# Beta/alpha product of a DeltaNet layer: activations as the stationary operand, 16 columns streamed

## The chip, the cores and the metric

One core of a Trainium2 chip runs the whole program. The metric is the device time in microseconds. Before the change the median of 3 runs was 1533.15 us, the lowest 1530.92 us and the highest 1536.06 us.

## The reference, cut to what matters

Two groups of tokens, 512 latent and 128 context tokens (640 together), pass two layers of a hybrid network of width 1024. The first layer has a bidirectional gated DeltaNet beside a short gated convolution, then a gated feed-forward part; the second has a pooling mixer and the same kind of feed-forward part. In the first layer one projection `w_in` feeds everything:

```python
p = h @ w_in                                  # h (tokens, 1024)
beta  = sigmoid(p[..., GATE_END:BETA_END])    # 2 directions x 4 heads = 8 columns
alpha = p[..., BETA_END:ALPHA_END]            # 8 columns
g = -exp(a_log) * softplus(alpha + dt_bias)
```

The change concerns these 16 columns only. All arrays are float32. `beta` and `g` are needed with one token per partition (five tiles of 128 tokens), because they scale and decay tokens of the scans.

## The kernel before, in words

Activations are kept with the channels on the partitions: `h` is eight blocks `k` of 128 channels by 640 tokens. To keep float32 accuracy each operand is split in two parts of the type fp32r: `hhi` and `hlo` for the activations, `whi` and `wlo` for the weights. A product is the sum of hi*hi, lo*hi and hi*lo over the eight blocks.

The projection is cut into 28 units of 128 output columns. A unit (`in_unit`, through `products`, L661 to L674) is 8 blocks x 3 part products x 2 halves of 320 tokens, so 48 matmuls whose stationary operand is a 128x128 piece of weights and whose moving operand is 320 tokens. The results alternate between the PSUM pairs A and B. While TensorE works on unit u, ScalarE takes the result of unit u-1 out of PSUM (L1085), VectorE runs the convolution over it (L1485 to L1494), and both split the weights of a later unit (L1098 and L1552). Each engine runs its own list of instructions in the order written, and semaphores tie the lists together; there is no planner.

The 16 beta/alpha columns have weights of their own, `wba_hi` and `wba_lo` (128 x 8 x 16). `beta_alpha` (L722) is issued on TensorE behind unit 5. It makes 48 matmuls with 16 columns of weights and 320 moving tokens, and leaves 16 partitions x 640 tokens in PSUM pair C. VectorE copies that to `acc` (L1561) between the work for units 5 and 6. Behind unit 7 TensorE transposes it in five pieces (`beta_alpha_tokens`, L732, the transposes stand on L736) into bank 7 of PSUM, 16 columns for each of the five token tiles. From there VectorE reads it (L1575, L1576) behind its loop over the first eight units, and the gate steps go on in `gates`. The semaphore `s_bat` counts the product, `s_gd` counts VectorE's gate steps (the copy is its first), `s_ba` says that bank 7 holds the result.

Behind the units 8 to 11 stand sums of squares for the q and k norms (`qk_sums`, L748). Behind unit 12 stand the gate sums (`gate_sums`, L759 and L761: six matmul records with 20 or 40 moving columns), and from unit 14 on products of k and q of one token tile (`grams`, L778) and decay rows (L768). A plain float32 matmul is one instruction in the code and two records in the trace.

Of the kernel before, what the change touches and what calls it, by code (L numbers as in the profile page):

```python
# [26 lines left out]
P = 128  # L27
D = 1024
KD = D // P
# [6 lines left out]
HALF = W // 2  # L36
# [11 lines left out]
TILES = [S0 + P * t for t in range(SEQ_S // P)] + [P0]  # L48
# [10 lines left out]
ALU = mybir.AluOpType  # L59
# [37 lines left out]
U_B, U_V, U_G = NQK, NQK + 3 * NB, NQKV + 3 * NB  # L97
BA_AFTER, GSUM_AFTER = 5, U_B + 4
# [46 lines left out]
def build(nc, t):  # L145
    ctx = ExitStack()
    with ctx:
        def sb(name, shape, dt=F32):
            return ctx.enter_context(nc.sbuf_tensor(name, shape, dt))

        def sem(name):
            return ctx.enter_context(nc.semaphore(name))
# [16 lines left out]
        wba_hi = sb("wba_hi", [P, KD, 16], F32R)  # L169
        wba_lo = sb("wba_lo", [P, KD, 16], F32R)  # L170
# [6 lines left out]
        ident, tri_u, tri_l, ones = (const[:, j, :] for j in range(4))  # L177
# [9 lines left out]
        acc = work[:, 8, :]  # L187
# [23 lines left out]
        hhi = nc.alloc_sbuf_tensor_at("hhi", [P, KD, W], F32R, offset=off_h)  # L211
        hlo = nc.alloc_sbuf_tensor_at("hlo", [P, KD, W], F32R, offset=off_h + size_h // 2)
# [48 lines left out]
        ps = ctx.enter_context(nc.psum_tensor("ps", [P, 8, 512], F32))  # L261
        pair = {n: ps[:, 2 * j:2 * j + 2, 0:HALF] for j, n in enumerate("ABCX")}
        bank = [ps[:, j, :].rearrange("p (h e) -> p h e", h=NH) for j in range(8)]

        def halves(ap):
            return ap.rearrange("p (b n) -> p b n", b=2)

        def col(name, pattern=None, **dims):
            a, n = COLS[name]
            v = cols[:, a:a + n]  # L270
            return v.rearrange(pattern, **dims) if pattern else v
# [76 lines left out]
        s_l2ln = sem("qk_logs")  # L348
        s_l2r = sem("qk_rsqrt")
        s_l2 = sem("qk_normed")  # L350
        s_bat = sem("beta_alpha_rows")
        s_ba = sem("beta_alpha_products")
        s_ga = sem("gate_steps_scalar")
        s_gd = sem("gate_steps_vector")
# [50 lines left out]
        def scan_tile(c, s):  # L405

            return NT - 1 if s == NT - 1 else (s if c == 0 else NT - 2 - s)

        def attn_of(n, c):

            return 2 * PREP.index(n) + c
# [248 lines left out]
        def _(pe):  # L660
# [56 lines left out]
            def in_unit(u, half_u, s, wait_k=None):  # L717
                pe.wait_ge(s_split, u + 1)
                pe.wait_ge(s_ev["AB"[s]], half_u + PRIMED)
                products("AB"[s], s, range(KD), hhi, hlo, range(KD), wait_k).then_inc(s_unit, 1)  # L720

            def beta_alpha():  # L722

                pe.wait_ge(s_mod, 1)
                for k in range(KD):
                    for q, (a, b) in enumerate(((wba_hi, hhi), (wba_hi, hlo), (wba_lo, hhi))):
                        for h in range(2):
                            last = nc.tensor.matmul(pair["C"][0:16, h], a[:, k, :], b[:, k, h * HALF:(h + 1) * HALF],
                                                    start=(k == 0 and q == 0), stop=(k == KD - 1 and q == 2))
                last.then_inc(s_bat, 1)  # L730

            def beta_alpha_tokens():  # L732

                pe.wait_ge(s_gd, 1)
                for tl, c0 in enumerate(TILES):
                    last = nc.tensor.transpose(ps[:, 7, 16 * tl:16 * tl + 16], acc[0:16, c0:c0 + P],  # L736
                                               ident[0:16, 0:16])
                last.then_inc(s_ba, 1)

            def qk_sums(m):  # L740

                pe.wait_ge(s_l2sq, m + 1)
                if m == 1:
                    pe.wait_ge(s_gd, 2)
                if m >= 2:
                    pe.wait_ge(s_l2ln, m - 1)
                for b in range(2):
                    last = nc.tensor.matmul(pair["CX"[m % 2]][:, b], ones, sq[m % 2][:, b * HALF:(b + 1) * HALF],  # L748
                                            start=True, stop=True)
                last.then_inc(s_l2sum, 1)  # L750
# [31 lines left out]
            for u in range(28):  # L782
                in_unit(u, u // 2, u % 2, (lambda j: pe.wait_ge(s_h, PRIMED + j + 1)) if u == 0 else None)
                if u == BA_AFTER:
                    beta_alpha()
                if u == U_B - 1:
                    beta_alpha_tokens()
                for m in L2_AFTER.get(u, ()):
                    qk_sums(m)
                if u == GSUM_AFTER:  # L790
                    gate_sums()
                if u in GRAMS_AFTER:
                    if GRAMS_AFTER[u] == 0:
                        pe.wait_ge(s_l2, 8)
                    for first in (4, 0):
                        grams(GRAMS_AFTER[u], first)
                if u in DECAYS_AFTER:
                    if DECAYS_AFTER[u] == 0:
                        pe.wait_ge(s_ga, 8)
                        pe.wait_ge(s_masks, 2)  # L800
                    for c in range(2):
                        decay_rows(DECAYS_AFTER[u], c)
# [65 lines left out]
            for s in range(NT):  # L868
                for c in range(2):
                    tl = scan_tile(c, s)  # L870
                    c0 = TILES[tl]
# [17 lines left out]
                    for h in range(NH):  # L889
                        last = nc.tensor.matmul(bank[b0 + 1][:, h], qkv[:, h, c0:c0 + P], S[:, h],  # L890
                                                start=True, stop=True)
                    last.then_inc(s_kq[c], 1)
                for c in range(2):
                    tl = scan_tile(c, s)
                    pe.wait_ge(s_r[c], s + 1)
                    for h in range(NH):
                        last = nc.tensor.matmul(bank[4 * c][:, h], rinv[:, 2 * tl + c, h], rr[c][:, h],
                                                start=True, stop=True)
                    last.then_inc(s_tr3[c], 1)
                for c in range(2):  # L900
                    tl = scan_tile(c, s)
# [6 lines left out]
                    for h in range(NH):  # L908
                        last = nc.tensor.matmul(bank[4 * c + 3][:, h], attn_kept[attn_of(tl, c)][:, h], vn[c][:, h],
                                                start=True, stop=True)  # L910
                    last.then_inc(s_ap[c], 1)

            for n in range(NT):
# [3 lines left out]
                for h in range(NH):  # L917
                    last = nc.tensor.transpose(bank[O_BANKS[n % 4]][:, h], osum[:, done_order[n], h], ident)
# [23 lines left out]
            for layer in range(2):  # L942
# [39 lines left out]
                for g, nf in enumerate(GROUPS):  # L982
                    b = SEG["up", layer, g]
# [401 lines left out]
        def _(dve):  # L1385
# [170 lines left out]
            dve.wait_ge(s_silu_rows, 1)  # L1556
            for u in range(NQK):
                s = u % 2
                if u == BA_AFTER + 1:
                    dve.wait_ge(s_bat, 1)  # L1560
                    nc.vector.tensor_copy(halves(acc)[0:16], pair["C"][0:16]).then_inc(s_gd, 1)  # L1561
                dve.wait_ge(s_ev["AB"[s]], u // 2 + (PRIMED + 1))
                dve.wait_ge(s_silu, u - s + PRIMED)
                conv(pad[s], cv[s], [tap_qkv[:, j, u:u + 1] for j in range(3)])
                weight_lo(u + 2)
                for _ in range(ROWS_IN[u]):
                    row_sums(rows)
                    rows += 1

            dve.wait_ge(s_ba, 1)  # L1570
            bav = ps[:, 7, 0:16 * NT].rearrange("p (t j) -> p t j", t=NT)

            def tiles(v):
                return v.rearrange("p (t j) -> p t j", t=NT)
            nc.vector.tensor_tensor(tiles(soft), bav[:, :, 8:16], tiles(col("dt_bias")), ALU.add)  # L1575
            nc.vector.tensor_scalar(tiles(lnbeta), bav[:, :, 0:8], -1.0, None, ALU.mult).then_inc(s_gd, 1)  # L1576

            def gate_logs():
# [208 lines left out]
            for s in range(NT):  # L1787
                for c in range(2):
                    tl = scan_tile(c, s)
                    dve.wait_ge(s_kq[c], s + 1)  # L1790
                    for h in range(NH):
                        j = tl * 8 + c * NH + h
                        last = nc.vector.scalar_tensor_tensor(
                            out=rr[c][:, h], in0=bank[4 * c][:, h], scalar=negegc[:, j:j + 1],
                            in1=vtok[:, tl, h], op0=ALU.mult, op1=ALU.add)
                    last.then_inc(s_r[c], 1)
                for c in range(2):
                    tl = scan_tile(c, s)
                    S = ss[:, c] if s < NT - 1 else sp_[:, c]
                    dve.wait_ge(s_ap[c], s + 1)  # L1800
                    for h in range(NH):
                        j = tl * 8 + c * NH + h
                        last = nc.vector.scalar_tensor_tensor(
                            out=S[:, h], in0=S[:, h], scalar=etot[:, j:j + 1], in1=bank[4 * c + 2][:, h],
                            op0=ALU.mult, op1=ALU.add)
                    last.then_inc(s_st[c], 1)
                for c in range(2):
                    tl = scan_tile(c, s)
# [28 lines left out]
            for n in range(NT):  # L1837
                c0 = TILES[done_order[n]]
# [25 lines left out]
            for layer in range(2):  # L1864
                if layer == 1:
# [6 lines left out]
                    for m in range(KD):  # L1872
                        dve.wait_ge(s_mix, m + 1)
                        for c0, n, cd in RANGES:
                            last = nc.vector.scalar_tensor_tensor(
                                out=x[:, m, c0:c0 + n], in0=ps[:, MIX_BANKS[m % 2][cd], 0:n],
                                scalar=mod[:, 1, 2, m, cd:cd + 1], in1=x[:, m, c0:c0 + n],
                                op0=ALU.mult, op1=ALU.add)
# [4 lines left out]
                for g, nf in enumerate(GROUPS):  # L1883
                    b = SEG["up", layer, g]
                    u, f = b["u"], b["f"]
# [169 lines left out]
```

## Time and profile before

| | |
|---|---|
| runs, median (lowest to highest) | 1533.15 us (1530.92 to 1536.06) |
| profiled execution, its own time | 1536.84 us |
| its span | 1535.0 us |
| TensorE matmul / weight load busy | 1411.7 us (92%) / 1371.1 us (89%) |
| VectorE, GpSimd, ScalarE busy | 980.9, 569.4, 433.5 us |
| mean granted TensorE clock | 0.974 |

The engines are named PE (TensorE matmul), PEld (TensorE weight load), DVE (VectorE), ACT (ScalarE), POOL (GpSimd). Matmuls are pipelined: the records of matmuls that follow each other overlap, so the time that one takes is read from the distance of the starts. In a merged row with a count, that distance is (length of the row less the length of one record) / (count less one). The granted clock is given as a share of 2.4 GHz; 0.50 is 1.2 GHz.

### The profile page before, as it was taken

The page shows a single profiled execution, that of the slowest core. Times are in us where ns is not written, and L with a number is a line of the kernel's source. Part 1 is how long each engine was busy: PE and PEld are TensorE (multiplying, and loading weights), DVE is VectorE, ACT ScalarE, POOL GpSimd, SP SyncE. Part 2 cuts the span into 40 slices and gives each one's busy share as a digit, 9 for nine tenths or more (in the row PEclk, how much of TensorE's full clock was granted, in tenths as well). Part 3 has the DMA queues.
Part 4 walks back from the last instruction along what each step waited for, and adds up shares of the span by engine and source line. Part 5 has one row for each costly group of instructions (what it writes and reads, how often), then busy time and mean ns, then how long its engine had stood idle before and what let it go on. Part 6 is the DMA issues. An engine that isn't in the chain of part 4 may idle for free.

```text
span 1535.0 us, 24664 instructions
## 1 busy us (share of the span) xinstructions
PE 1411.7 (92%) x9517; PEld 1371.1 (89%) x9517; DVE 980.9 (64%) x1403; ACT 433.5 (28%) x744; POOL 569.4 (37%) x348
## 2 busy tenths in 40 slices
PE   2699999989879799999999999897999999999995
PEld 1499989988878799999999999776999999999995
DVE  5774688887664677778888886445654155325554
ACT  4744442454421533101100111346331011001122
POOL 0200010003225355555556555212545454455542
PEclk9899999999999899999999999997999999999998
DMA  9242212353032245334344332111332222222222
GB/s 372 113 143 92 97 56 69 113 191 134 15 127 76 75 137 186 122 132 141 123 141 161 137 112 83 65 41 35 103 123 69 82 69 80 67 79 76 68 72 79
DMA packets 44791, 163.24 MB, mean 106 GB/s; under 512 B 4800, under 2 KB 5952, under 8 KB 43584
## 3 DMA queue, kind: packets, MB, share of 16 engines
q1 hardware_dynamic: 44736, 162.52, 30.5%
q8 instruction: 32, 0.52, 0.1%
q14 instruction: 23, 0.19, 0.0%
HBM read 154.12 MB, written 6.82 MB: 105 GB/s over the span
## 4 chain that ended last, share of the span: by engine, by line
PE 71%; DVE 15%; issue 6%; ACT 6%; DMA 2%; ACTq 0%; POOL 0%; DVEq 0%; SPq 0%; POOLq 0%
PE ps L670 61%; DVE ada_raw L1471 3%; PE ps L955 2%; DVE junk L1471 1%; DVE work L1488 1%; DVE work L1494 1%; ACT work L1024 1%; DVE work L1485 1%; ACT work L1170 1%; PE ps L682 1%; DMA x<-in_x 1%; DVE work L1893 1%; PE ps L778 1%; ACT work L1377 1%; DMA work<-in_zeros 1%
## 5 line engine op out<-in xcount | busy, mean ns | idle before, releaser
L670 PE MATMUL ps<-hhi,whi 128*128 128x320 f32 x1984 | 459.9, 313 | 40.5 <-DVE hlo L1455 31.6
L670 PE MATMUL ps<-hlo,whi 128*128 128x320 f32 x1984 | 454.4, 310 | 0.0
L670 PE MATMUL ps<-hhi,wlo 128*128 128x320 f32 x1984 | 454.0, 310 | 0.0
L599 POOL TENSOR_SCALAR whi<-raw 128x1024 fp32r<-128x1024 f32 (+1 forms) x146 | 161.0, 1103 | 621.0 <-PE ps L670 528.0
L602 POOL TENSOR_TENSOR wlo<-raw,whi 128x1024 fp32r<-128x1024 f32 (+1 forms) x146 | 374.5, 2565 | 12.2
L670 PEld LDWEIGHTS ps<-hhi,whi 128*128 128x128 f32 x1984 | 333.7, 190 | 50.0 <-issue 20.8
L670 PEld LDWEIGHTS ps<-hlo,whi 128*128 128x128 f32 x1984 | 334.5, 190 | 0.0
L670 PEld LDWEIGHTS ps<-hhi,wlo 128*128 128x128 f32 x1984 | 334.0, 189 | 0.0
L670 PE MATMUL ps<-hidhi,whi 128*128 128x320 f32 x704 | 161.3, 310 | 2.8 <-DVE hidlo L1896 2.8
L670 PE MATMUL ps<-hidlo,whi 128*128 128x320 f32 x704 | 161.1, 310 | 0.0
L670 PE MATMUL ps<-hidhi,wlo 128*128 128x320 f32 x704 | 161.1, 310 | 0.0
L1471 DVE SCALAR_TENSOR_TENSOR ada_raw<-ada_raw,cond_rows 128x1024 bf16<-128x1024 f32 x70 | 140.1, 2002 | 0.0
L1485 DVE TENSOR_SCALAR work<-work,cols 128x640 f32<-128x640 f32 x60 | 67.2, 1120 | 104.3 <-ACT work L1374 86.9
L670 PEld LDWEIGHTS ps<-hidhi,whi 128*128 128x128 f32 x704 | 118.5, 189 | 3.1 <-DVE hidlo L1896 3.1
L1374 ACT ACTIVATE work<-ps 128x640 f32<-128x640 f32 x44 | 31.0, 704 | 315.2 <-PE ps L670 315.0
L670 PEld LDWEIGHTS ps<-hidlo,whi 128*128 128x128 f32 x704 | 118.4, 189 | 0.0
L670 PEld LDWEIGHTS ps<-hidhi,wlo 128*128 128x128 f32 x704 | 118.4, 189 | 0.0
L1488 DVE SCALAR_TENSOR_TENSOR work<-work,cols 128x511 f32<-128x511 f32 x120 | 99.1, 866 | 3.7 <-DVE work L1485 0.3
L1896 DVE TENSOR_TENSOR hidlo<-work,hidhi 128x640 fp32r<-128x640 f32 (+1 forms) x44 | 74.5, 1693 | 41.2 <-ACT hidhi L1379 41.2
L1471 DVE SCALAR_TENSOR_TENSOR junk<-ada_raw,cond_rows 128x1024 bf16<-128x1024 f32 x70 | 90.5, 1292 | 1.9 <-DVE ada_raw L1471 0.5
L1426 DVE SCALAR_TENSOR_TENSOR x<-ps,mod,x 128x320 f32<-128x320 f32 (+2 forms) x120 | 45.4, 434 | 71.6 <-PE ps L670 71.6
L1377 ACT ACTIVATE work<-work 128x640 f32<-128x640 f32 x44 | 32.5, 739 | 198.6 <-DVE work L1494 198.4
(205 smaller groups left out, 1353.1 us busy)
## 6 DMA issues: line engine op xcount, KB each, us to landing
raw<-in_w_gu SPq DMA_DIRECT2D x88, 512.0 KB, 3.2
ada_raw<-in_w_rows SPq DMA_DIRECT2D x70, 512.0 KB, 3.6
raw<-in_w_in SPq DMA_DIRECT2D x28, 512.0 KB, 3.3
raw<-in_w_dn SPq DMA_DIRECT2D x32, 448.0 KB, 3.4
ada_first<-in_w_ada SPq DMA_DIRECT2D x4, 2048.0 KB, 22.6
raw<-in_w_dn SPq DMA_DIRECT2D x16, 512.0 KB, 3.3
row_late<-in_w_rows SPq DMA_DIRECT2D x10, 512.0 KB, 3.3
raw<-in_w_out SPq DMA_DIRECT2D x8, 512.0 KB, 4.2
```

The lines of the kernel that those rows point to most:

```text
L599: nc.gpsimd.tensor_scalar(whi[s][:, 0:n], raw[s][:, 0:n], 1.0, 0.0, ALU.mult, ALU.add).then_inc(s_whi, 1)
L602: nc.gpsimd.tensor_tensor(wlo[s][:, 0:n], raw[s][:, 0:n], whi[s][:, 0:n].bitcast(F32), ALU.subtract).then_inc(s_split, 1)
L670: last = nc.tensor.matmul(pair[pr][:, b], wt[s][:, cs], act[:, k, b * HALF:(b + 1) * HALF], start=(j == 0 and q == 0), stop=(j == len(tile ...
L682: last = nc.tensor.matmul(ada_row(n), c_parts[:, q, 4 * s + k, :], w[:, k * ADA_COLS:(k + 1) * ADA_COLS], start=(s == 0 and k == 0 and q = ...
L955: last = nc.tensor.matmul(ps[:, bk, 2 * P * e:2 * P * (e + 1)], h_mix[:, 2 * g + kk, at:at + P], w_mix[:, g, kk, :], start=(kk == 0), stop ...
L1374: nc.scalar.activation(halves(pad[0]), pair["A"], ACT.Copy).then_inc(s_ev["A"], 1)
L1377: nc.scalar.activation(cv[1], cv[0], ACT.Silu).then_inc(s_silu, 1)
L1426: last = nc.vector.scalar_tensor_tensor(out=x[:, k, xc:xc + ln], in0=pair[n][:, bk, pc:pc + ln], scalar=mod[:, layer, 3 * part + 2, k, cd: ...
L1471: last = nc.vector.scalar_tensor_tensor(out=(row_out(n), row_buf(n)[:, 0:SLOT // 2].bitcast(mybir.dt.bfloat16))[c], in0=row_buf(n), scalar ...
L1485: own.tick(nc.vector.tensor_scalar(dst[:, 0:W], src[:, 0:W], taps[1], None, ALU.mult))
L1488: last = nc.vector.scalar_tensor_tensor(out=dst[:, c0 + 1:c0 + n], in0=src[:, c0:c0 + n - 1], scalar=taps[0], in1=dst[:, c0 + 1:c0 + n], o ...
L1896: nc.vector.tensor_tensor(hidlo[:, i, :], h32[0], hidhi[:, i, :].bitcast(F32), ALU.subtract).then_inc(s_hid, 1)
```

## The change

`beta_alpha` now takes a piece of the activations, 128 channels x 128 tokens, as the stationary operand and streams the 16 columns of `wba_hi` or `wba_lo`. Each of the five token tiles takes 8 blocks x 3 part products, 120 matmuls together, and writes its 16 columns of bank 7 directly, with tokens on the partitions. `beta_alpha_tokens`, VectorE's copy and the semaphore `s_bat` are gone. The first of VectorE's two gate steps (the addition of `dt_bias`) raises `s_gd` in place of the copy, so that the later counts stay as they were.

```diff
@@ -722,19 +721,11 @@
             def beta_alpha():
 
                 pe.wait_ge(s_mod, 1)
-                for k in range(KD):
-                    for q, (a, b) in enumerate(((wba_hi, hhi), (wba_hi, hlo), (wba_lo, hhi))):
-                        for h in range(2):
-                            last = nc.tensor.matmul(pair["C"][0:16, h], a[:, k, :], b[:, k, h * HALF:(h + 1) * HALF],
+                for tl, c0 in enumerate(TILES):
+                    for k in range(KD):
+                        for q, (b, a) in enumerate(((hhi, wba_hi), (hlo, wba_hi), (hhi, wba_lo))):
+                            last = nc.tensor.matmul(ps[:, 7, 16 * tl:16 * tl + 16], b[:, k, c0:c0 + P], a[:, k, :],
                                                     start=(k == 0 and q == 0), stop=(k == KD - 1 and q == 2))
-                last.then_inc(s_bat, 1)
-
-            def beta_alpha_tokens():
-
-                pe.wait_ge(s_gd, 1)
-                for tl, c0 in enumerate(TILES):
-                    last = nc.tensor.transpose(ps[:, 7, 16 * tl:16 * tl + 16], acc[0:16, c0:c0 + P],
-                                               ident[0:16, 0:16])
                 last.then_inc(s_ba, 1)
@@ -783,8 +774,6 @@
                 if u == BA_AFTER:
                     beta_alpha()
-                if u == U_B - 1:
-                    beta_alpha_tokens()
@@ -1556,9 +1545,6 @@
                 s = u % 2
-                if u == BA_AFTER + 1:
-                    dve.wait_ge(s_bat, 1)
-                    nc.vector.tensor_copy(halves(acc)[0:16], pair["C"][0:16]).then_inc(s_gd, 1)
                 dve.wait_ge(s_ev["AB"[s]], u // 2 + (PRIMED + 1))
@@ -1572,7 +1558,7 @@
-            nc.vector.tensor_tensor(tiles(soft), bav[:, :, 8:16], tiles(col("dt_bias")), ALU.add)
+            nc.vector.tensor_tensor(tiles(soft), bav[:, :, 8:16], tiles(col("dt_bias")), ALU.add).then_inc(s_gd, 1)
```

## Rows read from the trace of the kernel before

**Rows 1.** The page: shares of the chain of work that ended last.
```profile
PE 71%; DVE 15%; issue 6%; ACT 6%; DMA 2%; ACTq 0%; POOL 0%; DVEq 0%; SPq 0%; POOLq 0%
```

**Rows 2.** That chain in order of time, 113 to 145 us: start, length, what.
```profile
113.60 7.03 PE ps L728 x48
120.63 14.08 PE ps L670 x96
134.71 0.41 PE ps L736 x5
135.12 7.24 PE ps L670 x48
```

**Rows 3.** Busy time by engine around the product: stretch, length, busy (records), clock.
```profile
113.30:120.50 7.20, 7.20 (x52) 4.74 (x51) 3.83 (x8) 2.39 (x3) 0.00 (x0) 1.00 0.44 139
120.50:127.60 7.10, 7.10 (x50) 7.10 (x50) 0.81 (x1) 0.00 (x0) 0.00 (x0) 1.00 0.06 23
```

**Rows 4.** VectorE in order of time: start, length, operation, idle before it.
```profile
120.67 0.81 DVE L1561 COPY work<-ps 16x640 f32<-16x640 f32 x1 [2.50 <-PE ps L728]
128.44 0.56 DVE L1485 TENSOR_SCALAR work<-work,cols 128x640 f32<-128x640 f32 x1 [6.96 <-ACT work L1085]
139.19 0.20 DVE L1575 TENSOR_TENSOR gates<-ps,cols 128x40 f32<-128x40 f32 x1
```

**Rows 5.** Who TensorE waited for, 105 to 300 us: total, times, longest.
```profile
PE ps L778 <- DVE qkv L1597: 2.5, 1, 2.5
```

**Rows 6.** Weight loads by shape: busy, mean ns of one.
```profile
L670 PEld LDWEIGHTS ps<-hhi,wlo 128*128 128x128 f32 x1984 | 334.0, 189 | 0.0
...
L728 PEld LDWEIGHTS ps<-hhi,wba_hi 128*16 128x16 f32 x16 | 1.5, 95 | 0.8
...
L769 PEld LDWEIGHTS ps<-below,ident 128*128 128x128 bf16 x10 | 1.0, 98 | 2.4 <-issue 2.4
```

**Rows 7.** Weight loads in order of time, clock 1.00, three places.
```profile
368.51 0.97 PEld L887 LDWEIGHTS ps<-ss,qkv 128*128 128x128 f32 x8 [1.51 <-issue]
...
178.83 0.56 PEld L759 LDWEIGHTS ps<-gates,const 128*128 128x128 f32 x4
179.31 0.30 PEld L761 LDWEIGHTS ps<-gates,const 128*128 128x128 f32 x2
179.53 0.30 PEld L670 LDWEIGHTS ps<-hhi,whi 128*128 128x128 f32 x2
...
134.63 0.39 PEld L736 LDWEIGHTS ps<-const,work 16*128 16x128 f32 x5 [0.19 <-issue]
```

**Rows 8.** Weight loads in order of time, at clock 0.50.
```profile
198.59 3.39 PEld L778 LDWEIGHTS ps<-qkv 128*128 128x128 f32 x16 [2.81 <-DVE qkv L1597]
```

**Rows 9.** Stretches that end as the clock falls, and some behind them.
```profile
196.05:198.40 2.35, 0.00 (x0) 0.00 (x0) 2.35 (x4) 2.35 (x10) 0.00 (x0) 1.00 0.62 223
198.60:201.80 3.20, 3.20 (x15) 3.20 (x16) 2.30 (x3) 1.22 (x3) 0.00 (x0) 0.50 0.04 12
201.80:205.00 3.20, 3.20 (x15) 2.01 (x15) 2.84 (x8) 2.59 (x10) 1.64 (x2) 1.00 0.42 152
...
494.17:498.78 4.61, 1.35 (x5) 0.68 (x4) 0.10 (x1) 4.31 (x6) 2.52 (x2) 1.00 0.19 52
...
498.78:505.60 6.82, 1.15 (x4) 1.18 (x5) 4.51 (x6) 5.60 (x10) 0.00 (x0) 0.50 0.50 196
...
1030.98:1034.67 3.69, 1.13 (x4) 0.68 (x4) 2.63 (x5) 0.96 (x2) 0.00 (x0) 1.00 0.00 0
...
1517.51:1522.78 5.27, 1.35 (x4) 0.68 (x4) 0.09 (x1) 4.99 (x7) 0.00 (x0) 1.00 0.01 2
```

**Rows 10.** Dense stretches at clock 0.50 until it rises, and one behind.
```profile
504.45:509.02 4.57, 4.54 (x16) 4.14 (x17) 3.95 (x6) 4.34 (x9) 0.00 (x0) 0.50 0.00 0
...
1045.71:1051.74 6.03, 5.93 (x21) 5.53 (x22) 5.09 (x7) 5.66 (x11) 0.00 (x0) 0.50 0.00 0
1051.74:1056.00 4.26, 3.00 (x17) 2.21 (x15) 2.37 (x4) 4.07 (x8) 0.00 (x0) 1.00 0.02 4
```

More of the change, by code:

```diff
@@ L350, in build @@
         s_l2 = sem("qk_normed")
-        s_bat = sem("beta_alpha_rows")
         s_ba = sem("beta_alpha_products")
```

## The prediction

> **What bounds the kernel now.** I read the shares of the chain first: TensorE holds 71% of the chain that ended last [rows 1]. Then the chain in order of time around the changed place [rows 2]: it never leaves TensorE from the product (7.03 us, 48 matmuls) over two units (14.08 us) and the five transposes (0.41 us) into the next unit. The busy times say the same: TensorE fills all 7.20 us and 7.10 us of the two stretches at clock 1.00, while VectorE works 3.83 and 0.81 us and ScalarE 2.39 and 0.00 us [rows 3]. The list of waits has for TensorE between 105 and 300 us one entry, 2.5 us [rows 5]. So what TensorE gains or loses behind unit 5 goes to the end one for one, unless a later wait takes it up. That one wait is for VectorE's norm of q and k, which hangs on sums issued on TensorE behind units 8 to 11, so it moves along with TensorE and takes up nothing.
>
> **The change part by part.**
>
> *Removed on TensorE:* the product, 7.03 us; the transposes, 0.41 us; and the slower start of the unit behind them, 7.24 us [rows 2] where 14.08 / 2 = 7.04 us is usual, so 0.20 us. Together 7.64 us. TensorE's wait for VectorE's copy lies within these.
>
> *Removed on VectorE:* the copy, 0.81 us. It is worth nothing: VectorE waited 2.50 us before it and 6.96 us behind it, the latter for unit 6's result [rows 4]. The readers of bank 7 (L1575, at 139.19 us) stand behind the loop over eight units and come some 4 us after the transposes were done, so that the result's being ready earlier brings nothing either; they wait for nothing new. The moved count of `s_gd` holds: the sums for the second q tile need the value 2, which both gate steps now give together. No DMA is added or moved, and SyncE's and GpSimd's lists keep their order.
>
> *Added on TensorE:* 120 pairs of a weight load (128 columns) and a matmul with 16 moving columns. In the old product one pair took 7.03 / 48 = 0.146 us and the matmul's 320 columns set it. With 16 columns the load must set it. A load of fp32r weights with 128 columns is recorded with 189 ns, with 16 columns 95 ns [rows 6], so 94 ns for 112 columns, 0.84 ns each, or 107 ns for 128. The distance of the starts agrees: eight float32 loads with 128 columns in 0.97 us make (0.97 - 0.19) / 7 = 0.111 us; and the nearest rows by moving columns, six pairs with 20 or 40 of them, take from 178.83 to 179.53 us, 0.117 us each [rows 7]. So a pair costs 0.111 us at the full clock, taking the longer series of equal pairs. The bounds from rows at that clock: below, the loads of the transposes, (0.39 - 0.14) / 4 = 0.062 us a pair [rows 7], with 16 rows; above, the 0.146 us of today. They give 7.4 and 17.6 us for the 120; 0.111 gives 13.3 us.
>
> Were the clock to stay at 1.00, the sum would be 13.3 - 7.64 = +5.7 us.
>
> *The clock.* It does not stay, I think. The rows before four of the trace's nine falls from 1.00 to 0.50 (2.4 GHz to 1.2) show TensorE with few moving columns: no matmul for 2.35 us, or four or five records in 3.69 to 5.27 us, 1.13 to 1.35 us of it busy [rows 9]. In the new product the array streams 16 columns each 0.111 us, where a unit streams 320 each 0.147 us: 7% of the columns of today, over 13 us. Only the weight loads would be dense. The trace has no stretch with dense loads and sparse columns, so whether loads alone hold the clock up is open, and I bound it from both sides: not at all (+5.7 us) and at 0.50 throughout.
>
> At 0.50 sixteen loads take (3.39 - 0.19) / 15 = 0.213 us each [rows 8], so 120 pairs take 25.6 us. The clock does not fall at once. The rows put the fall 2.35 to 5.27 us behind the last dense work; the four mean 4.0 us. By then 4.0 / 0.111 = 36 pairs are done, and the other 84 take 84 x 0.213 = 17.9 us: 21.9 us together (20.5 to 23.5 us for the ends). Then unit 6 begins at 0.50. The rows show dense work at 0.50 for 3.2, 4.57 and 6.03 us until the clock rises [rows 9, 10]; the mean is 4.6 us and half of it, 2.3 us, is lost (1.6 to 3.0 us). The sum: 21.9 + 2.3 - 7.64 = +16.6 us, with ends 20.5 + 1.6 - 7.6 = +14.5 and 23.5 + 3.0 - 7.6 = +18.9 us.
>
> The Trainium skill bears on this in "TensorE: Matmul & The Clock Gate", Part 4 (PE-mode transpose): it says that transposes do not count as PE-busy in the way that makes the chip give the full clock. Its "What's actually happening" has activity release the throttle, without saying that weight loads are activity. No row here tests loads alone; if a load counts like a matmul, the sum is the +5.7 us above, if it doesn't, the +16.6 us.
>
> Forecast: the profiled execution's 1536.84 us becomes 1553.4 us. The median of the runs lies 3.7 us below that execution, and against it the time is 1533.15 + 16.6 = 1549.8 us.
>
> **The rivals.**
>
> *A: the dense loads hold the clock at 1.00.* For it: TensorE is never idle in the product, and the falls in the rows all come with much idle time. Against it: before three of those four falls TensorE was not wholly idle [rows 9], and a load moves no columns. It gives +5.7 us, 1538.8 us (up to +10 us if a pair costs 0.146 us).
>
> *B: not slower.* One mechanism: the fp32r loads of the new product go faster than 0.111 us a pair. From 7.64 / 120 = 0.064 us down the change is no loss. For it: loads with 128 columns and 16 rows come each 0.062 us, and a bf16 load with 128 columns is recorded with 98 ns, hardly over one with 16 columns [rows 6, 7]. Against it: these have another type or few rows, and the same activations' type as weights (L670) shows 189 ns. At 0.062 us it gives 7.4 - 7.64 = -0.2 us, 1533 us, if the shorter stretch also spares the clock. The skill's section "Fast Weight Load" of the same page says that the fast load needs a type other than FP32, which would speak against B if fp32r counts as FP32; and its "Back-to-back issue gap" has about 81 ns for a sustained pair with 128 columns, which would give 9.7 us for the 120, +2.1 us; the 0.111 us of the trace stand against that.
>
> *C: the pairs cost more than a load.* If fp32r with few moving columns is run as two passes with two loads, as a plain float32 matmul is, 240 loads come to 26.6 us at 1.00 and up to 51 us at 0.50: +19 to +46 us, 1552 to 1579 us. For it: each float32 instruction has two records. Against it: the old product's 48 fp32r matmuls have 48 records [rows 2], with 320 columns each.
>
> **How the numbers follow.** The clock falls: 0.68. A: 0.19. B: 0.05. C: 0.08. The likeliest gives 1550 us, its own range 1546 to 1555 us (the ends +14.5 and +18.9 us, and some 2 us for the spread of a median over the runs, 1530.92 to 1536.06). The 8-in-10 range goes down to A: 1537 to 1556 us; it leaves out B, most of C and A's lowest edge. A measurement of this kernel can tell about 0.3%, 4.6 us, from no change. A's +5.7 us lies near that bound, so a third of A counts as the same, with B's greater part: same 0.10, faster 0.03, slower 0.87.
>
> **What would show it.** In the new profile the product should be 120 matmul records with 128x16 moving, none of L736 or L1561. The clock shown for that stretch should be 1.00 for its first 2.4 to 5.3 us, with load starts 0.11 us apart, then 0.50 with 0.213 us. The whole should take some 22 us, and unit 6 behind it over 7.04 us. VectorE's wait for unit 6's result should grow from 6.96 us by the same amount. TensorE's wait before L778 should stay near 2.5 us. If the clock stays at 1.00 throughout, A holds. If loads stand under 0.1 us apart at 1.00, B. If there are 240 records, C. If the product takes 22 us and the time does not grow by some 14 us, the claim that nothing behind it takes up the delay is wrong.

## The result

The changed kernel takes 1551.3 us (median of 4 runs, 1546.88 to 1551.88) where the one before took 1534.4 us in the same runs (1530.92 to 1536.06): a ratio of 1.0107, 95% interval 1.0080 to 1.0134, so it is slower by some 16 us. In the profiled execution of the changed kernel, which took 1546.88 us, its span 1545.1 us, TensorE's mean granted clock is 0.967 (0.974 before).

The chain that ended last shows the place. This is that chain of the changed kernel, in order of time: start, length, what.

```profile
113.00 22.66 PE ps L727 x120
135.65 23.15 PE ps L669 x144
```

The product (now L727) takes 22.66 us where it took 7.03 [rows 2]. The three units behind it (L669, 144 matmuls; nothing stands between the second and the third any longer) take 23.15 us, where three units at the full clock take 21.1.

The clock shows why. The first view has the busy time by engine and the granted clock (third number from the end) of four stretches of the changed kernel; the second its weight loads where the clock falls: start, length, operation.

```profile
112.83:115.89 3.06, 3.06 (x31) 3.06 (x29) 2.05 (x4) 1.65 (x2) 0.00 (x0) 1.00 0.64 216
115.89:135.65 19.76, 19.76 (x95) 19.76 (x94) 1.67 (x3) 0.74 (x1) 0.00 (x0) 0.50 0.08 27
135.65:139.79 4.14, 4.14 (x17) 4.14 (x17) 0.00 (x0) 0.00 (x0) 0.00 (x0) 0.50 0.02 4
139.79:145.00 5.21, 5.21 (x37) 5.21 (x36) 0.00 (x0) 0.23 (x1) 0.00 (x0) 1.00 0.00 0
```

```profile
115.74 0.19 PEld L727 LDWEIGHTS ps<-wba_hi,hhi 128*128 128x128 f32 x1
115.85 0.29 PEld L727 LDWEIGHTS ps<-wba_hi,hlo 128*128 128x128 f32 x1
116.02 0.34 PEld L727 LDWEIGHTS ps<-wba_lo,hhi 128*128 128x128 f32 x1
116.24 0.33 PEld L727 LDWEIGHTS ps<-wba_hi,hhi 128*128 128x128 f32 x1
116.45 0.33 PEld L727 LDWEIGHTS ps<-wba_hi,hlo 128*128 128x128 f32 x1
```

For 3.06 us from the product's first matmul (112.83 us) the loads come 0.111 us apart at 2.4 GHz. Then the clock goes to 1.2 GHz, the recorded load from 0.19 to 0.33 us, and the distance to 0.213 us. TensorE counts as 100% busy in all four stretches, before the fall and behind it: the busy share alone says nothing here, and the clock beside it says everything. The clock comes back 4.14 us after the units began again. VectorE and ScalarE have next to nothing to do in 24 us; VectorE's wait for unit 6's result is now 27.95 us.

```profile
145.50 0.56 DVE L1474 TENSOR_SCALAR work<-work,cols 128x640 f32<-128x640 f32 x1 [27.95 <-ACT work L1074]
```

The wait grows by 21.0 us. Before, the copy parted it into 2.50 us, the copy's own 0.81 us and 6.96 us [rows 4], 10.3 us together; against these the growth is 17.7 us, which is the longer product (15.6 us) and the slower unit 6 (2.0 us).

Compared by the ends of units, unit 5 ends 0.6 us earlier than in the trace of before, and unit 8 ends 16.4 us later: the place costs 17.0 us in the profiled execution. That execution was the fastest of four. By its own time it is only 10.0 us over the profiled execution of before, for reasons that lie elsewhere in the program (last section).

### The profile page after: what moved, and what is told of

The parts are those of the page before. It is cut to its first block, busy times and chain, and to the rows that moved or that the text cites. A ratio compares the mean times of both kernels' runs of the same rounds, so it can differ in the third digit from the quotient of the medians.

```text
span 1545.1 us, 24797 instructions
## 1 busy us (share of the span) xinstructions
PE 1428.6 (92%) x9584; PEld 1390.8 (90%) x9584; DVE 975.9 (63%) x1402; ACT 433.4 (28%) x744; POOL 569.9 (37%) x348
## 4 chain that ended last, share of the span: by engine, by line
PE 71%; DVE 15%; ACT 5%; issue 5%; DMA 1%; ACTq 0%; POOL 0%; DVEq 0%; SPq 0%; POOLq 0%
PE ps L669 60%; DVE ada_raw L1460 3%; PE ps L944 1%; DVE junk L1460 1%; PE ps L727 1%; DVE work L1477 1%; DVE work L1483 1%; DVE work L1474 1%; ACT work L1013 1%; ACT work L1159 1%; PE ps L681 1%; DVE work L1879 1%; PE ps L769 1%; DMA x<-in_x 1%; ACT work L1366 1%
## 5 line engine op out<-in xcount | busy, mean ns | idle before, releaser
L669 PE MATMUL ps<-hhi,whi 128*128 128x320 f32 x1984 | 460.5, 314 | 38.5 <-DVE hlo L1444 31.3
L669 PE MATMUL ps<-hlo,whi 128*128 128x320 f32 x1984 | 455.1, 311 | 0.0
L669 PE MATMUL ps<-hhi,wlo 128*128 128x320 f32 x1984 | 454.8, 310 | 0.0
L669 PEld LDWEIGHTS ps<-hhi,whi 128*128 128x128 f32 x1984 | 334.9, 190 | 47.6 <-issue 20.8
L669 PEld LDWEIGHTS ps<-hlo,whi 128*128 128x128 f32 x1984 | 335.4, 190 | 0.0
L669 PEld LDWEIGHTS ps<-hhi,wlo 128*128 128x128 f32 x1984 | 334.9, 190 | 0.0
L669 PE MATMUL ps<-hidhi,whi 128*128 128x320 f32 x704 | 160.5, 309 | 0.1
L669 PE MATMUL ps<-hidlo,whi 128*128 128x320 f32 x704 | 160.4, 309 | 0.0
L669 PE MATMUL ps<-hidhi,wlo 128*128 128x320 f32 x704 | 160.3, 309 | 0.0
L1474 DVE TENSOR_SCALAR work<-work,cols 128x640 f32<-128x640 f32 x60 | 63.8, 1063 | 126.8 <-ACT work L1363 88.3
L1460 DVE SCALAR_TENSOR_TENSOR ada_raw<-ada_raw,cond_rows 128x1024 bf16<-128x1024 f32 x70 | 136.2, 1946 | 0.0
L669 PEld LDWEIGHTS ps<-hidhi,whi 128*128 128x128 f32 x704 | 117.8, 188 | 0.3 <-DVE hidlo L1882 0.3
L669 PEld LDWEIGHTS ps<-hidhi,wlo 128*128 128x128 f32 x704 | 117.9, 188 | 0.0
L669 PEld LDWEIGHTS ps<-hidlo,whi 128*128 128x128 f32 x704 | 117.7, 188 | 0.0
L1477 DVE SCALAR_TENSOR_TENSOR work<-work,cols 128x511 f32<-128x511 f32 x120 | 105.1, 917 | 3.7 <-DVE work L1474 0.3
```

Source lines behind the costliest of these rows:

```text
L669: last = nc.tensor.matmul(pair[pr][:, b], wt[s][:, cs], act[:, k, b * HALF:(b + 1) * HALF], start=(j == 0 and q == 0), stop=(j == len(tile ...
L1460: last = nc.vector.scalar_tensor_tensor(out=(row_out(n), row_buf(n)[:, 0:SLOT // 2].bitcast(mybir.dt.bfloat16))[c], in0=row_buf(n), scalar ...
L1474: own.tick(nc.vector.tensor_scalar(dst[:, 0:W], src[:, 0:W], taps[1], None, ALU.mult))
L1477: last = nc.vector.scalar_tensor_tensor(out=dst[:, c0 + 1:c0 + n], in0=src[:, c0:c0 + n - 1], scalar=taps[0], in1=dst[:, c0 + 1:c0 + n], o ...
```

## The experiments

All ran beside the kernel before, whose median was 1534.7 us in the first four and 1535.3 us in the other three.

**The changed kernel once more**, with no edit.

> The changed kernel once more, beside the kernel before. Theory (the clock falls in the stretch of bare weight loads): some 17 us over the kernel before; in the profile the 120 pairs take 20.5 to 23.5 us, their load starts 0.111 us apart until the granted clock goes to 0.50, and 0.213 us from there on, the fall standing 2.3 to 5.3 us into the product. Rival (the fall seen once was a chance of that execution): a clock of 1.00 through the product, 13.3 us for it and +5.7 us.

Measured: 1550.7 us, ratio 1.0107 (1.0088 to 1.0126). The chain, and by it the product:

```profile
115.18 21.14 PE ps L727 x120
136.31 23.05 PE ps L669 x144
```

The clock stands at 1.00 for the first 4.73 us of the product and at 0.50 from there to 3.92 us into unit 6:

```profile
115.02:119.75 4.73, 4.73 (x46) 4.73 (x44) 3.72 (x6) 2.39 (x3) 0.00 (x0) 1.00 0.42 138
119.75:136.31 16.56, 16.56 (x80) 16.56 (x79) 0.00 (x0) 0.00 (x0) 0.00 (x0) 0.50 0.10 32
136.31:140.23 3.92, 3.92 (x16) 3.92 (x16) 0.00 (x0) 0.00 (x0) 0.00 (x0) 0.50 0.01 4
```

In the other execution the fall stood at 3.06 us; 1.6 us more at 0.111 us a pair spare 1.5 us of the whole. So the cost differs with the place of the fall, within the range expected: from the product's start to the end of unit 8 this execution takes 15.4 us more than before, the other 17.0 us. Both traces have the fall.

**Eight times the columns.** Each matmul streams its 16 columns eight times over:

```diff
-last = nc.tensor.matmul(ps[:, 7, 16 * tl:16 * tl + 16], b[:, k, c0:c0 + P], a[:, k, :],
+last = nc.tensor.matmul(wide[tl], b[:, k, c0:c0 + P],       # wide: (r=8, j=16) of bank 7 or 6
+                        a[:, k, :].unsqueeze(1).to_broadcast([P, 8, 16]),
```

> The changed kernel with the same 120 loads, but each matmul streams its 16 columns eight times over (128 moving columns, into eight columns groups of PSUM of which the first is read). Nothing else differs but four small reads in place of two. Theory (the clock falls because few columns are streamed): the added columns fit under a load (about 0.05 us of streaming in 0.111 us), the clock stays at 1.00, the product takes 13.3 us instead of 22.7 and the kernel is 5.7 us over the one before, so about 11 us under the changed one although it streams eight times the columns. Rival (a long series of fp32r loads is slow or drops the clock by itself): no gain over the changed kernel, +17 us, and the clock at 0.50 in the product.

Measured: 1538.6 us, ratio 1.0032 (1.0017 to 1.0047) to the kernel before: some 12 us faster than the changed kernel, with the same loads and more arithmetic. The chain of this kernel and the clock of the product:

```profile
112.45 13.35 PE ps L729 x120
125.80 21.17 PE ps L669 x144
```

```profile
112.30:125.60 13.30, 13.30 (x122) 13.30 (x121) 3.71 (x6) 2.39 (x3) 0.00 (x0) 1.00 0.27 90
```

The product takes 13.35 us, 0.111 us a pair, the units behind it 21.17 us, and the clock is 1.00 throughout. Weight loads as dense as in the changed kernel did not drop the clock; with them dense in both, what differs is how many columns the matmuls move and, with them, how many results they write. No run parts these two. This is the run that parts the two terms of the sum: 120 loads instead of 48 matmuls, and the clock.

**The pairs beside dense matmuls**, one behind each matmul of units 5 to 7:

```diff
@@ products
                             last = nc.tensor.matmul(pair[pr][:, b], wt[s][:, cs], ...)
+                            if beside is not None:
+                                beside()                     # one load and one 16-column matmul
@@ the loop over units
-                if u == BA_AFTER:
-                    beta_alpha()
+                in_unit(..., ba_pair if u >= BA_AFTER else None)
```

> The changed kernel with the same 120 pairs, one behind each matmul of units 5 to 7 in place of all behind unit 5. Theory (a pair costs its load, 0.111 us at the full clock, and the 11 us on top are the clock's): the unit's dense matmuls beside keep it at 1.00, units 5 to 7 take 3 x 7.04 + 13.3 = 34.4 us, and the kernel is 5.7 us over the one before. Rival 1 (loads hide under the unit's matmuls, which have 0.036 us each to spare): units 5 to 7 take under 30 us and the kernel is faster than before by up to 2 us. Rival 2 (not the clock): +17 us as the changed kernel.

Measured: 1541.2 us, ratio 1.0052 (1.0032 to 1.0072), so +8 us with an interval from 5 to 11. The clock over the three units and the loads within one:

```profile
105.00:139.50 34.50, 34.50 (x267) 34.50 (x266) 16.09 (x28) 7.18 (x9) 0.00 (x0) 1.00 0.29 100
```

```profile
109.91 0.19 PEld L669 LDWEIGHTS ps<-hhi,whi 128*128 128x128 f32 x1
110.02 0.19 PEld L730 LDWEIGHTS ps<-wba_hi,hhi 128*128 128x128 f32 x1
110.17 0.19 PEld L669 LDWEIGHTS ps<-hhi,whi 128*128 128x128 f32 x1
```

From one load of the unit to the next there are 0.26 us, as much as 0.147 for the unit's matmul and 0.111 for the pair: the pair costs its full price beside the unit's matmul, although that leaves 0.036 us beyond its own load. Why nothing of it hides was not tried. From the first matmul of unit 5 to that of unit 8 there are 34.3 us (105.39 to 139.73), where 34.4 us were expected and the kernel before, transposes included, has 28.65 us (106.40 to 135.05): 5.7 us more. The first rival is out, and the second by the clock.

**The old product twice**: `for _ in range(2):` around the old layout's loops, 48 dense matmuls more at the same place.

> The kernel before with its product computed twice, 96 matmuls of 320 columns, so 7.03 us more of dense TensorE work at the same place and no change of the clock. Theory (what TensorE gains or loses there goes to the end one for one): +7.0 us. Rival (a later wait takes part of it up): +0 to +5 us, and TensorE's waits behind unit 8 are shorter in the profile than before.

Measured: 1542.1 us, ratio 1.0043 (1.0027 to 1.0059), so +6.6 us, from 4.1 to 9.1. In its profile the units from 6 on lie 7.2 us later than before, 0.2 us of which was there ahead of the product, and what stands behind the scans lies 6.8 us later. TensorE's waits behind unit 8, and the second of them as the kernel before has it:

```profile
PE ps L779 <- DVE qkv L1598: 2.5, 1, 2.5
PE ps L839 <- DVE work L1688: 2.2, 1, 2.2
```

```profile
PE ps L838 <- DVE work L1687: 3.2, 1, 3.2
```

The first is as it was [rows 5]. The second, in the scans, is 1.0 us shorter, which is the rival's sign; but the delay behind the scans is only 0.3 to 0.4 us less. Nearly all of it is passed on, and the rival's 0 to 5 us are left only in the part from 4.1 us up.

**Two products beside**: the run before last, with the hi activations loaded once for hi and lo weights.

```diff
-ba_pairs = [... for k in range(KD) for q in range(3)]
+ba_pairs = [... for k in range(KD) for q in range(2)]
-                b, a = ((hhi, wba_hi), (hlo, wba_hi), (hhi, wba_lo))[q]
+                b, n = ((hhi, 32), (hlo, 16))[q]             # moving: wba[:, k, 0:n]
```

> The change's layout with its pairs beside the matmuls of units 5 to 7 as in the run before it, and with two products in place of three: the hi activations stay loaded and stream 32 columns, the hi and the lo weights side by side, the lo activations stream 16, and VectorE adds the two parts. 80 pairs in place of 120. Theory (the price of this layout is the number of its loads, 0.111 us each at the full clock): units 5 to 7 take 21.1 + 8.9 = 30.0 us, and the kernel is 8.9 - 7.64 = 1.2 us over the one before, 4.4 us under the kernel with 120 pairs beside. Rival (the price is the streamed columns or something fixed): no nearer to before than that kernel, +5 to +8 us.

Measured: 1534.3 us, ratio 0.9998 (0.9985 to 1.0012). From the first matmul of unit 5 to that of unit 8 its profile has 29.9 us (104.67 to 134.59), the clock at 1.00 throughout. That is 4.4 us less than with 120 pairs beside (34.3) and 1.3 us more than before (28.65), both as expected. By the medians, forty loads fewer brought more, 8.3 us (both intervals taken together, about 4.6 to 12); the profiles show 4.4 of it at this place. So the layout of the change, with the clock kept and a third of the loads gone, is as fast as the kernel before, and no faster.

**The old product within unit 0**, whose blocks wait for the split activations:

```diff
+BA_BLOCKS = {2: (0,), 3: (1, 2), 4: (3,), 5: (4, 5), 7: (6, 7)}   # behind block j of unit 0
-                if u == BA_AFTER:
-                    beta_alpha()
```

> The kernel before with its own layout, where the product's blocks are computed between the blocks of unit 0, in which TensorE waits for the split activations: block 0 behind block 2 of the unit, 1 and 2 behind 3, 3 behind 4, 4 and 5 behind 5, 6 and 7 at the end. Theory (time of TensorE counts one for one where it is never idle, and less where it waits): the 48 matmuls fill gaps of 0.3 to 1.2 us each; worked out block by block from the starts in the trace, unit 0 and the product end some 3.4 us after the end of unit 0 today and not 7.03 us, so 3.6 us faster than before. Rival (the gaps are not free because the later blocks are held up as well): 0 to 2 us faster.

Measured: 1532.5 us, ratio 0.9985 (0.9971 to 1.0000), some 2.3 us faster, at most 4.5. The 3.6 us lie in the interval, and so does all of the rival; not settled by the time. The profile has no wait of TensorE left inside unit 0 except the one before its first block. From the first matmul of unit 0 to that of unit 8 it has 66.2 us (61.37 to 127.56), before 69.3 us (65.71 to 135.05): 3.1 us less, nearer to the 3.6 us than to the rival's 0 to 2. That is one execution of each kernel, with the clock at 0.50 for the first 4.7 us of this stretch here and 3.0 us before.

**The same with two products**, 32 weight columns (hi and lo) against the hi activations and 16 against the lo:

```diff
-for q, (a, b) in enumerate(((wba_hi, hhi), (wba_hi, hlo), (wba_lo, hhi))):
+for q, (n, b) in enumerate(((32, hhi), (16, hlo))):
     for h in range(2):
-        nc.tensor.matmul(pair["C"][0:16, h], a[:, k, :], ...)
+        nc.tensor.matmul(pair["C"][0:n, h], wba[:, k, 0:n], ...)
@@ beta_alpha_tokens
-nc.tensor.transpose(ps[:, 7, ...], acc[0:16, c0:c0 + P], ident[0:16, 0:16])
+nc.tensor.matmul(ps[:, 7, ...], acc[0:32, c0:c0 + P], col("eye2")[0:32], start=True, stop=True)
```

> As the run with the product in unit 0, in the layout of before, and with two products in place of three: 32 weight columns, hi and lo side by side, against the hi activations, and 16 against the lo activations, 32 matmuls in place of 48; the five transposes become small matmuls with a stacked identity, which add the two parts. Theory: 0.59 us a block in place of 0.88, so that nearly all lies in the gaps: unit 0 and the product end 1.2 us after unit 0 today, the small matmuls cost 0.3 to 0.6 us more than the transposes, and the kernel is 5.5 us faster than before. Rival (as above): 2 to 4 us faster, no more than the 2.3 us that the 16 matmuls are worth and a little for the gaps.

Measured: 1528.5 us, ratio 0.9962 (0.9947 to 0.9977), so 5.8 us faster than the kernel before, from 3.5 to 8.1. The 5.5 us expected lie well within, but the upper end of the rival (2 to 4 us) does too. This is the fastest of all. In its list of waits from 58 to 300 us TensorE waits for the first block of unit 0, and then 2.5 us as before [rows 5]. This is the line of the first:

```profile
PE ps L670 <- DVE hlo L1459: 8.7, 1, 8.7
```

In the kernel before, this line has 11.2 us in five waits: four of them, 2.5 us together, are filled now. The small matmuls that add the parts cost more than I had put down, 1.28 us in ten records where the five transposes took 0.41 us in the chain [rows 2]:

```profile
128.32 1.28 PE L741 MATMUL ps<-cols,work 32*128 32x16 f32 x10
```

The stretch from unit 0 to unit 8 takes 65.3 us here (64.26 to 129.53), 4.1 us less than before and not 5.5. In this execution the clock was at 0.50 for the first 6.0 us of it, where it was so for 3.0 us before; how much of the difference that is was not tried.

## Why the prediction was right

The forecast was +16.6 us by a sum of four terms. This is each of them against the changed kernel's profile.

| term | forecast | measured |
|---|---|---|
| removed on TensorE | 7.64 us | 7.6 us (28.76 us before from the product's start to the end of unit 8, less the 21.17 us of the three units in the run with 128 columns) |
| a pair at 1.00 | 0.111 us | 0.111 us, and 13.35 / 120 in the run with 128 columns |
| the fall, behind the product's start | 4.0 us (2.35 to 5.27) | 3.06 us, and 4.73 us in the second execution |
| a pair at 0.50 | 0.213 us | 0.213 us |
| the product | 21.9 us (20.5 to 23.5) | 22.66 and 21.14 us |
| lost in the units behind | 2.3 us (1.6 to 3.0) | 23.15 - 21.17 = 2.0 us and 23.05 - 21.17 = 1.9 us, the clock back after 4.14 and 3.92 us |
| passed on to the end | all | +6.6 us (4.1 to 9.1) for 7.03 us of dense work; 1.2 us less behind the scans in both traces of the changed kernel |

The mechanism is the one forecast. That the sum, +16.6 us, meets the difference of the medians, 16.9 us, to 0.3 us is partly luck: the interval runs from +12.3 to +20.6 us, the place cost 17.0 us in one execution and 15.4 us in the other, and the 0.8 us by which the product was put too low in the first stand against 0.3 us too much for the units behind. The forecast for the profiled execution, 1553.4 us, missed by 6.5 us (last section). One end of the range was summed wrongly: a fall after 5.27 us leaves 72.5 pairs, so 20.7 us for the product and not 20.5, which changes no bound by more than 0.2 us.

- *The load sets the price of a pair.* Right. The nearest rows were float32 loads with other operands [rows 7], and the fp32r loads behaved as these did, to the nanosecond. Rival B needed 0.064 us a pair; in the new product no load of any trace came closer to the next one than 0.085 us, and at 2.4 GHz the usual distance was 0.111 us. The bf16 row of 98 ns and the transposes' 0.062 us were poor guides for this type: the recorded length of the kernel's own fp32r loads, 189 ns [rows 6], was the better one. The Trainium skill's "TensorE: Matmul & The Clock Gate" says in "Weight-path perf modes — Fast Weight Load (FWL) and DoubleRow" that FP32 weights get no fast load, and the fp32r loads of this trace, 0.111 us apart and recorded with 0.19 us like the float32 loads of L887 (192 ns), agree with being counted as such. The same page's "Back-to-back issue gap" has about 81 ns for a sustained pair with 128 moving columns; in the run with 128 columns a pair took 0.111 us.
- *The clock falls in the product.* Right, and this was the step that decided: 11 of the 17 us are the clock's. The rows of before did not show dense loads with sparse columns; the forecast took the side that the stretches ahead of the falls pointed to, few moving columns. The run with 128 columns shows that it was the right side: with dense loads in both, more columns kept 2.4 GHz and fewer lost it. In the Trainium skill, "What's actually happening" on the same page has activity release the throttle and leaves open what counts; here loads with 16-column matmuls did not hold it and loads with 128-column matmuls did.
- *Rival A* (the loads hold the clock) had the price right, +5.7 us, for a kernel in which the clock is kept: the runs with 128 columns and with the pairs beside the units are that case, +4.9 us (2.6 to 7.2) and +8.0 us (4.9 to 11.1). Only the condition was wrong for the change as made.
- *Rival C* (two records a pair) is out: 120 records.
- *Nothing that leaves VectorE brings anything.* Right: VectorE stood idle for 27.95 us at that place, and the readers of bank 7 (L1561, L1562) ran at 156.25 us, behind their loop as before.
- *No later wait takes it up.* Right up to 300 us: the wait before L769 is 2.5 us in the changed kernel, as [rows 5] had it. But the list of waits behind that claim ended there, and the scans behind it hold one more, for VectorE, shown above for the kernel before with 3.2 us. In both traces of the changed kernel it is 2.0 us:

```profile
PE ps L827 <- DVE work L1673: 2.0, 1, 2.0
```

Over the scans the changed kernel's lag goes from 16.4 to 15.2 us in one trace and from 16.9 to 15.7 us in the other. So 1.2 us were taken up there, which the forecast had at nothing. Whether the delay itself shortens the wait is not shown: it is 2.1 us in the fastest kernel too, which comes there earlier than the kernel before. And in the runs with 128 columns and with the pairs beside the units the lag grows by 1.0 us over the same stretch, though the wait is shorter by 0.9 and 1.0 us; the clock fell once more there (at some 323.4 us, for 3.4 us).

What stays open: why the medians of the two runs with the pairs beside the units lie 8.3 us apart, when the 40 loads are 4.4 us of it in the profiles; and how much the place in unit 0 gives by itself (2.3 us, from 0 to 4.5).

## What to carry to other kernels

Count weight loads, not matmuls, where the moving operand is short: here a 128-column fp32r load came each 0.111 us at 2.4 GHz with 16 and with 128 columns moving behind it, and making the wide operand the stationary one turned 48 matmuls of 0.147 us into 120 loads of 0.111. Ask of every stretch that streams few columns what the granted clock will do in it, even when TensorE is 100% busy there, and price the stretch and the dense work right behind it at both levels. A small product is worth trying where TensorE waits anyway, and its hi and lo weights side by side save a whole pass: that pair of edits gave 5.8 us in the old layout, where the place alone gave 2.3 us, not clearly told from nothing. Look for later waits over the whole rest of the program, not over a part of it.

## What the runs showed that I had not expected

Executions of one kernel differ by a single wait. In the profiled executions of the kernel before and of the changed kernel's second profile, TensorE waits 2.8 us for `hidlo` in the feed-forward part of the program and the clock is at 0.50 for 3.4 us behind it (631.9 to 635.3 us before); this is the line of the first, in the waits from 600 to 660 us:

```profile
PE ps L670 <- DVE hidlo L1896: 2.8, 1, 2.8
```

The changed kernel's first profile has neither, and there its lag behind the kernel before shrinks from 15.2 to 10.9 us. With the 1.2 us at the scans and some 0.8 us in small steps behind, that is why this execution is 10 us over the profiled one of before, where the medians are 17 us apart. Why the wait is missing there was not tried.
